# Key pages moved ahead of the prompt's attention, and the value pages interleaved with it, in a decoder-layer kernel

## What is computed

```
mod = silu(c) @ w_ada + b_ada                      # shift, scale, gate, twice
h = rms_norm(x) * (1 + scale1) + shift1
q, k, v, (GLA inputs), gates = h @ w_in
q, k = rms_norm per head                            # 8 heads of 64
prompt: softmax(q k^T * scale + rel_bias, causal) v # 512 x 512 per head, 4 blocks of 128 queries
sample: per sequence 2048 past keys and values in 16 pages of 128 tokens (page_table),
        + its own 4; a gate per block of 256 keys picks the top 3 past blocks; softmax; times v
o_g = gated linear attention (GLA), 4 heads, chunks of 32
x = x + gate1 * ((sigmoid(ga) * (o_a @ w_branch_a) + sigmoid(gb) * (o_g @ w_branch_b)) @ w_out)
x = x + gate2 * mixture of 32 experts (2 of them per token, SwiGLU)
```

## Time and profile before

| what | us |
|---|---|
| median of three runs | 1698.22 |
| the profiled execution, its own time | 1696.8 |
| its span | 1695.1 |
| prompt's attention, 176.8 to 288.3 | 111.5 |
| key pages, 288.3 to 389.6 | 101.3 |
| value pages, 389.6 to 456.1 | 66.5 |
| from there to GLA's first matmul, 460.0 | 3.9 |
| TensorE busy | 1493.1 (88%) |
| DMA, mean of the span | 224 GB/s |

### The profile page before, as it was taken

The page is one execution under the profiler, slowest core; times in us unless marked ns, Lnnn a source line. Parts: engine busy times, 40 slices in busy tenths (PEclk is TensorE's granted clock), DMA queues, the critical chain, the costliest instruction groups (busy, mean ns, idle before and its releaser), DMA issues.

```text
span 1695.1 us, 20005 instructions
## 1 busy us (share of the span) xinstructions
PE 1493.1 (88%) x7656; PEld 907.4 (54%) x7656; DVE 364.3 (21%) x845; ACT 296.7 (18%) x591; POOL 206.2 (12%) x283
## 2 busy tenths in 40 slices
PE   7899999999699999999999999858888888888880
PEld 4344455884285858585888878633333333333330
DVE  2432453032014141414000001431010101010104
ACT  3100322672022212131000000510000000000001
POOL 2121300334201010101000010010000000000006
PEclk9899656999699989899999999979888989898995
DMA  9954600999961222222131026339999999999984
GB/s 342 339 200 149 185 16 1 336 327 373 367 188 54 68 72 69 68 72 72 44 94 50 0 80 221 126 118 389 405 394 404 400 404 398 400 402 398 414 347 164
DMA packets 126621, 379.34 MB, mean 224 GB/s; under 512 B 9492, under 2 KB 54677, under 8 KB 110158
## 3 DMA queue, kind: packets, MB, share of 16 engines
q1 hardware_dynamic: 105552, 308.44, 48.7%
q0 software_dynamic: 20016, 67.11, 12.0%
q10 hardware_dynamic: 974, 2.74, 0.4%
HBM read 352.69 MB, written 25.56 MB: 223 GB/s over the span
## 4 chain that ended last, share of the span: by engine, by line
PE 28%; DMA 21%; DVE 2%; ACT 1%; issue 1%; POOL 0%; SPq 0%; POOLq 0%; ACTq 0%; DVEq 0%
PE ps L1279 28%; DMA ring<-in_w_exp_up 20%; PE ps L1290 1%; DVE work L1273 0%; ACT work L741 0%; DMA xT<-expert_rows,dest_i 0%; SPq L408 0%; DVE work L1272 0%; ACT hT L596 0%; DMA hT<-h_rows,idx 0%; DVE work L1104 0%; POOL work L570 0%; DMA expert_rows<-xT 0%; POOLq L108 0%; POOL work L566 0%
## 5 line engine op out<-in xcount | busy, mean ns | idle before, releaser
L1279 PE MATMUL ps<-ring,hT 128*64 128x512 f32 (+4 forms) x2416 | 628.9, 586 | 78.5 <-DMA ring<-in_w_exp_up 56.6
L1279 PEld LDWEIGHTS ps<-ring,hT 128*64 128x64 f32 (+2 forms) x2416 | 283.2, 160 | 398.0 <-issue 348.3
L1279 PE MATMUL ps<-work 128*32 128x128 f32 (+10 forms) x1812 | 227.1, 342 | 27.7 <-DVE work L1223 9.4
L1279 PE MATMUL ps<-hT,ring 128*128 128x272 f32 x768 | 187.5, 407 | 0.5 <-ACT work L718 0.5
L1279 PEld LDWEIGHTS ps<-work 128*32 128x32 f32 (+6 forms) x1812 | 137.8, 142 | 88.8 <-issue 29.6
L1279 PEld LDWEIGHTS ps<-hT,ring 128*128 128x128 f32 x768 | 151.6, 198 | 34.8 <-issue 1.5
L1279 PE MATMUL ps<-work,ring 128*128 128x272 f32 x640 | 148.2, 393 | 2.3 <-POOL work L525 2.3
L1279 PEld LDWEIGHTS ps<-work,ring 128*128 128x128 f32 x640 | 121.5, 190 | 27.7 <-POOL work L525 2.7
L769 ACT ACTIVATE hT<-ps 128x256 f32<-128x256 f32 x32 | 12.3, 384 | 451.2 <-PE ps L1279 451.2
L1290 PEld LDWEIGHTS ps<-cst,work 128*128 128x128 f32 (+5 forms) x388 | 52.0, 179 | 60.3 <-issue 45.9
L1290 PE MATMUL ps<-cst,work 128*128 128x128 f32 (+5 forms) x388 | 71.9, 312 | 12.6 <-DVE work L1039 4.5
(11 more groups left out here) (266 smaller groups left out, 924.9 us busy)
## 6 DMA issues: line engine op xcount, KB each, us to landing
ring<-in_w_exp_gate SPq DMA_DIRECT2D x32, 2048.0 KB, 19.0
ring<-in_w_exp_up SPq DMA_DIRECT2D x32, 2048.0 KB, 24.4
ring<-in_w_exp_down SPq DMA_DIRECT2D x32, 2048.0 KB, 24.6
ring<-in_w_ada SPq DMA_DIRECT2D x12, 2048.0 KB, 20.4
ring<-in_cache_k SPq DMA_DIRECT2D x64, 256.0 KB, 4.5
ring<-in_cache_k POOLq DMA_DIRECT2D x64, 256.0 KB, 4.7
ring<-in_cache_v SPq DMA_DIRECT2D x64, 256.0 KB, 6.9
ring<-in_cache_v POOLq DMA_DIRECT2D x64, 256.0 KB, 5.7
```

The source lines that it names most:

```text
L1279: return pe.matmul(out, lhsT, rhs, start=start, stop=stop, **k)
```

## The change

The stages are put in another order. The key pages follow the q/k/v tiles at once, in the same form as before. Then comes one loop over the prompt's 32 units, in which the value pages' blocks stand at fixed turns: blocks 1 to 7 behind the scores of turns 1, 3, ... 13 and blocks 8 to 15 behind those of turns 20, 22, ... 34; block 0 stands ahead of the loop. The transposes of the second group's weights stand at turns 15 to 19, one quarter each, and `selected(0)` at turn 20. The maximum of the second group is taken by VectorE ahead of the loop, its exponential by ScalarE ahead of the loop, its scaling by VectorE at turn 1. The projection `gk` goes behind the loop.

Ring slot 5 is left out of the pages' turns (`SPARE`), so pages use five slots; it holds `kpage` during the key stage, and then `sc_p` and the turned weights `prT`. The next block that SyncE puts into it (`AFTER_SPARE`) waits for the last transposes of the prompt and the last value block. The first 16 of POOL's page DMAs stand ahead of the stores of v. The remaining buffers are carved anew, and the PSUM banks are dealt out anew, since both stages are now alive at once.

```diff
-        SLOT_ORDER = [0, 1, 2, 3, 4, 5, 0] + [1, 2, 3, 1, 2, 3, 1, 2] + [3, 4, 1, 2, 5, 0] * 9
+        SLOT_ORDER = [0, 1, 2, 3, 4, 5, 0] + [1, 2, 3, 1, 2, 3, 1, 2] + [3, 4, 1, 2, 0] * 6 + [3, 4] + [1, 2, 0, 5, 3, 4] * 3
+        SPARE = 5
...
+        kpage = grid(ring[:, SPARE, :], 8)
+        sc_p, prT = grid(ring[:, SPARE, 0:3 * 512], 3), grid(ring[:, SPARE, 2048:], PAGES)
...
+        VALUES_AT = {**{2 * v - 1: v for v in range(1, 8)}, **{2 * v + 4: v for v in range(8, 16)}}
+        TURN_AT, SELECT_AT = 15, 20
...
+                if n == AFTER_SPARE:
+                    sp.wait_ge(s("p_tr"), 32)
+                    sp.wait_ge(s("pv_s"), 2 * PAGES // 2)
...
+            pool.wait_ge(s("page_table_in"), 16)
+            for i in range(4):
+                half_pages("k", i)
             pool.wait_ge(s("v_ready"), 5)
             pool.dma_start(v_prompt[0, 0]...)
             pool.dma_start(v_sample[0]...)
+            for i in range(4, KEY_PAGES // 8):
+                half_pages("k", i)
+            for i in range(KEY_PAGES // 8):
+                half_pages("v", i)
...
 # ScalarE
+            for pg in range(KEY_PAGES):        # page copies, exponent(0) among them
...
+            weights(0, range(5))
+            exponent(1)
             for x in range(34):                # the prompt's units
...
+                if TURN_AT <= x < TURN_AT + 5:
+                    weights(1, [x - TURN_AT])
+                if x == SELECT_AT + 1:
+                    sample_heads(0)
+            sample_heads(1)
...
 # VectorE
             for n in range(QUADS // 4):
                 dve.wait_ge(s("page_sc"), 4 * n + 4)
                 dve.tensor_copy(logits[n // 4][...], ps[:, 4 + n % 2, :]).then_inc(s("sc_taken"), 1)
+                if n == 5:
+                    softmax_norm(0)
                 if n % 4 == 3:
-                    softmax(n // 4)
+                    softmax_max(n // 4)
...
+            for x in range(32 + 4):            # the prompt's units
+                if x == 1:
+                    softmax_norm(1)
+                if x == TURN_AT:
+                    sample_rows(0)
+            sample_rows(1)
...
 # TensorE
-            pe.wait_ge(s("qk_T"), NORMED)
+            pe.wait_ge(s("pj_free"), NORMED)
             pe.wait_ge(s("v_ready"), 5)
+            for quad in range(QUADS + 1):      # the key pages, own_scores() behind quad 0
...
+            weights_turned(0, range(5))
+            page_values(0)
+            pe.wait_ge(s("sc_taken"), QUADS // 4)
             for x in range(32 + 3):
...
+                if x in VALUES_AT:
+                    page_values(VALUES_AT[x])
+                if TURN_AT <= x < TURN_AT + 5:
+                    weights_turned(1, [x - TURN_AT])
+                if x == SELECT_AT:
+                    selected(0)
...
+            product(2, lambda k: wgk[:, k, :], lambda k: hT[:, k, :], KD, RANK).then_inc(*done("gk_ps"))
             selected(1)
             pe.wait_ge(s("oa_taken"), 2)
+            pe.wait_ge(s("p_ov"), 32)
```

More of the change, by code:

```diff
@@ L49 @@
 TAB = 384
-WORK = 16550
+WORK = 16580
 RBM = 255
@@ L1399, in _, with own_scores @@
                     ada(ada_after(n))
-            pe.wait_ge(s("qk_T"), NORMED)
-            pe.wait_ge(s("v_ready"), 5)
+            def own_scores():
+                pe.wait_ge(s("qk_T"), NORMED)
+                pe.wait_ge(*after("q_row"))
+                for b in range(DEC_B):
+                    r = slice(32 * (b % 4), 32 * (b % 4) + 32)
+                    for a in range(PAIRS):
+                        last = mm(ps[r, 3, NS * (b // 4):NS * (b // 4) + NS], q_row[:, a, b, :], kT[:, a, sample], a == 0, a == PAIRS - 1,
+                                  skip_group_check=True)
+                last.then_inc(*done("own_ps"))
@@ new lines, in _ @@
+            pe.wait_ge(s("pj_free"), NORMED)
+            pe.wait_ge(s("v_ready"), 5)
+            for quad in range(QUADS + 1):
+                if quad < QUADS:
+                    for pg in range(4 * quad, 4 * quad + 4):
+                        n = PAGED[("k", pg // 8)]
+                        landed(pe, n)
+                        if pg >= 3:
+                            pe.wait_ge(s("page_T"), pg - 2)
+                        for a in range(PAIRS):
+                            last = turn(ps[:, pg % 3, P * a:P * a + P], slot(n)[:, AW * (pg % 8) + P * a:AW * (pg % 8) + P * a + P])
+                        last.then_inc(s("page_tr"), 1)
+                if quad == 0:
+                    own_scores()
+                if quad:
+                    y = quad - 1
+                    g, page = y // PAGES, y % PAGES
+                    pe.wait_ge(s("page_T"), 4 * y + 4)
+                    if y == 0:
+                        pe.wait_ge(s("mod_set"), 2)
+                    if page % 4 == 0 and y >= 8:
+                        pe.wait_ge(s("sc_taken"), y // 4 - 1)
+                    for a in range(PAIRS):
+                        for j in range(4):
+                            last = mm(ps[32 * j:32 * j + 32, 4 + y // 4 % 2, P * (page % 4):P * (page % 4) + P], q_row[:, a, 4 * g + j, :],
+                                      kpage[:, (4 * y + j) % 8, P * a:P * a + P], a == 0, a == PAIRS - 1, skip_group_check=True)
+                    last.then_inc(s("page_sc"), 1)
@@ new lines, in weights_turned @@
+            def weights_turned(g, part):
+                pe.wait_ge(s("l_norm"), g + 1)
+                for q in part:
+                    if q >= 2 or g:
+                        pe.wait_ge(s("pr_T"), 5 * g + q - (0 if g else 1))
+                    if q == 4:
+                        last = turn(ps[0:NS, 6 if g else 7, 0:P], logits[g][:, PAST:])
+                    else:
+                        for page in range(4 * q, 4 * q + 4):
+                            last = turn(ps[:, 6 if g else (6, 1)[q % 2], P * (page % 4):P * (page % 4) + P], logits[g][:, P * page:P * page + P])
+                    last.then_inc(s("pr_tr"), 1)
@@ new lines, in page_values @@
+            def page_values(v):
+                g, i = v // (PAGES // 2), v % (PAGES // 2)
+                if i == 0:
+                    pe.wait_ge(s("pr_T"), 5 * g + 5)
+                    if g:
+                        pe.wait_ge(s("o_rows"), g)
+                    for j in range(4):
+                        mm(ps[32 * j:32 * j + 32, 0, :], pr_own[0:NS, 32 * j:32 * j + 32], v_tok[0:NS, PT, :], True, False,
+                           skip_group_check=True)
+                n = PAGED[("v", v)]
+                landed(pe, n)
+                for page in (2 * i, 2 * i + 1):
+                    for j in range(4):
+                        q = 4 * (page % 2) + j
+                        last = mm(ps[32 * j:32 * j + 32, 0, :], prT[:, page, 32 * j:32 * j + 32], slot(n)[:, AW * q:AW * q + AW],
+                                  False, page == PAGES - 1, skip_group_check=True)
+                last.then_inc(s("pv_s"), 1)
@@ new lines, in selected @@
+            def selected(g):
+                pe.wait_ge(s("o_rows"), g + 1)
+                if g:
+                    pe.wait_ge(s("oa_taken"), g)
+                else:
+                    pe.wait_ge(s("pr_T"), 10)
+                for a in range(PAIRS):
+                    at = 64 * g + 16 * a
+                    last = mm(ps[:, 6, at:at + 16], o_rows[g][:, P * a:P * a + P], const("row_token"), True, True)
+                last.then_inc(s("o_sel"), 1)
+            weights_turned(0, range(5))
```

251 lines of the change are left out of this document (84 added, 167 removed).

## The result

The changed kernel took 1639.09 us, the median of four runs (1647.88, 1630.99, 1647.07, 1631.10), beside 1697.55 us for the kernel before on the same chip. The ratio is 0.9659, 95% interval 0.9589 to 0.9729: faster, by 58 us. The prediction said 1640. The runs fall into two groups, near 1631 and near 1647; the profiled one is of the longer group, 1647.88 us.

The account below looks back on a forecast made before the run. Bound: TensorE at half clock, TensorE at full clock, then DMA, in a row. Keys to 274.6, passage to 288.8, loop to 390.5, end to 401.4: 58.6 us off 1696.8, stated as 1640; 8-in-10 range 1619 to 1672.

Parts of the forecast that it names:

- The bound: Three stages in a row before GLA: TensorE at half clock, TensorE at full clock, DMA; together 283.2 us.
- Part 1, keys: Key stage, now first: 32 quads of 3.01 us plus 1.5 from 176.8, ending at 274.6, pages not binding.
- Part 2, the passage: Between keys and loop: second group's softmax delays the first transposes 14.2 us, to 288.8; TensorE idles some 5.
- Part 3, the loop: Units with value blocks among them: bound by TensorE, 101.7 us, ending at 390.5.
- the 89 and the quarter: Loop: 89 us if all at full clock; half clock taken for a quarter of the stage's time.
- the 7.4 of the sum: Loop: four units at full clock taken as 7.4 us, where before they repeated in 13.66 at half clock.
- The argument for the share: Loop: value blocks raise the clock and waits for pages lose it; blocks are near except at turns 14 to 19.
- Part 4, the end: Behind the loop, `gk` 7.27 us in the open, 10.9 in all; GLA starts at 401.4, 58.6 us earlier.
- The sum: Whole kernel: 1696.8 less 58.6 gives 1638.2 us, 1639.6 on the medians' scale, stated as 1640.
- Half clock all through (1713): Loop takes 168 us instead of 101.7, GLA starts 15.3 us later than before: 1713 us, chance 0.09.
- Turns that serialise: Loop: VectorE and ScalarE stand still behind each block, 114 us: 1652 in all, within the forecast's range, no own chance.
- Full clock from start to end: Loop takes 84 us, GLA starts at 383, gain 77 us: 1621 us, chance 0.17.

Follow-up runs that it names:

- Order alone: Changed kernel with key pages still first, but value blocks 1 to 15 and the second weights behind the units' loop: 1715.35 us, ratio 1.0096.
- Clock alone, in before: Kernel before with eight dense matmuls of resident data, result unread, at each odd turn of its attention loop: 1683.90 us, ratio 0.9916.
- kernel with `gk` early: Changed kernel with the `gk` projection moved from behind the loop to turn 1: 1630.95 us; measured a second time, 1628.42 us.
- thin ones: Changed kernel with one matmul of eight left in 12 of the value blocks, sample's results wrong: 1637.22 us, ratio 0.963.
- Spreading the turns: Changed kernel with the second weights' transposes at turns 5, 8, 12, 14, 15 and blocks 8 to 15 at turns 17 to 31: 1634.3 us.

## Why the prediction was right

**The bound.** Right: the units' 110 us at half clock were the cost, and the change took half clock away from them. Order alone: 1% slower. Clock alone, in before: GLA 18 us earlier, with 16 useless blocks in the stage. The other 33.7 us up to GLA are there only when the blocks are the useful ones and their pages move under the units; how much of them each of the two is worth was not taken apart.

**Part 1, keys.** Predicted 97.8 us to an end at 274.6; measured 100.0 (179.28 to 279.3), a quad 3.01 us as said, no wait for pages. The 2.2 us are the one wait of 2.28 us for ScalarE at 252.78. Of it 0.86 stood in before's key stage too, and 32 x 3.01 has no place for it; 1.42 is the table load, which I had not counted either: I moved the softmax's exponential but not the table it needs. The Trainium skill ("ScalarE: Activation LUTs", What ACT_TABLE_LOAD costs) gives 2.66 us for each switch, load and drain together; here the load's row is 1.28 us and the wait grew by 1.42. The stage also began 2.5 us later than 176.8, but this is the spread of executions: in the two other profiles of after it begins at 176.53 and 176.09.

**Part 2, the passage.** Predicted 14.2, measured 14.0 (279.28 to 293.33), with 5.0 us of TensorE idle as said. What I left out is that those waits cost the clock: three of three profiles of after lose it there for 6.8 us, as do all four others without `gk` in the gap, and with `gk` in it none of four did.

**Part 3, the loop.** Predicted 101.7, as 89 us at full clock with a quarter of the time at half; measured 104.3, with 30.7 us, 29%, at half. The kernel with `gk` early ran the same loop wholly at full clock in 90.4 us, so both the 89 and the quarter were low. A third term was too high and took back part of it: half clock was priced at half of its time, and it cost 13.9 us (104.3 less 90.4) for about 30, and 10.7 us for 23.8 between the two profiles of the `gk` kernel. Part of TensorE's waits vanish at the low clock. Four units alone at full clock keep TensorE busy for 7.52 us but take 8.58, with a wait of 1.01; in the loop, 90.4 less 25.2 for blocks and 4.5 for the rest leaves about 7.6 for four, near the 7.4 of the sum. So at full clock the blocks fill time that TensorE alone would spend in waits, and this makes the interleaved loop shorter than its parts one behind the other.

The argument for the share was half right. Blocks do bring the clock back: with them it rose after 3.4 to 17 us, without them not until the last unit, in up to 109 us. But they need not be dense, since thin ones do it too. What in them does it stays open. It is not that they fill waits: at half clock the units alone had hardly any (85.84 of 87.00 us busy) and stayed there. The places I named, turns 14 to 19, are where it was lost. The wait there is a queue: ScalarE's copy of the turned weights (L646) starts at 333.65, behind an exponential of 512 columns at 332.67 and its copy, while TensorE wants the bank it empties. Spreading the turns cut the wait to 0.76 us and the half-clock time to 10.2.

**Part 4, the end.** Predicted 10.9, measured 10.56 (397.64 to 408.20), `gk` 7.51 for 7.27. Behind GLA's start, 1238.0 us against 1235.1 in before, said to be unchanged: 2.9 us more. In the other profiles this same code took from 1236 to 1246 us. Its first 600 us are the same to 0.1 us of TensorE's work, so that the spread lies behind them, in the router and the experts. There the clock falls and rises every few tens of microseconds, and TensorE also waits for the experts' matrices from the DMA, 55.2 us in all in after and 74.8 with thin blocks, the longest tail, where TensorE itself was busy for 12 us less. So it is not the clock alone. In five of the six profiles in which GLA began before 400 us it took 1242 us or more, in all eight others less. What sets it was not traced, and it hides part of what was won in the loop: the spread turns began GLA 14.6 us earlier and ended 8.8 earlier.

**The sum** of the misses: 2.5 and 2.2 in front, 2.6 in the loop, 2.9 behind, against 0.5 given back in passage and end: 9.7 us; 1638.2 became 1647.9 in the profiled run. The median hit 1640 because half of the runs are 16 us shorter. The prediction had put its number on one profiled execution and did not foresee the two groups. That it hit within 1 us is therefore luck; that the gain is the clock and the interleaving, of about this size, is not.

**The rivals.** Half clock all through (1713) did not come; that the order alone gives 1715 is a coincidence, since that kernel has its blocks behind the units. Turns that serialise did not come either: TensorE idles 3.3 of 104.3 us, in two waits for ScalarE, and four units keep their 7.6 us. Full clock from start to end came in one profile of the `gk` kernel, with 90.4 us for the loop where the rival had 84. The Trainium skill ("TensorE: Matmul & The Clock Gate", Part 4) would have transposes not count as work: the key stage, two thirds transposes, held 1.00 for 101 us with the units far off, so that the rule does not decide here.

**Open.** Where the runs of about 1631 us differ from those of 1647 was not seen in after itself, as all three profiles are of the longer group. The two profiles of the `gk` kernel differ by 12.9 us in time, 10.7 of them in the loop, where one has 23.8 us at half clock and the other none; this is the likely answer. Why a wait of 1.74 us costs the clock in one execution and not in the next the traces do not show. The Trainium skill (same page, Part 1) says that the monitor behind the clock runs free of the kernel, so that the same program changes clock at other points; the two profiles agree with that and do not prove it.

## What to carry to other kernels

A stage in which TensorE is 99% busy at half clock may be one that could run at full clock: ask whether matmuls that stand in another stage behind the DMA can be put among its own. To find out, put useless matmuls among its work once and see whether it gets shorter. In a stage that holds the clock, a wait of 1 to 2 us costs its own length and, some of the time, more: 3.4 to 17 us at half clock followed here, and 23.8 us of them made one loop 10.7 us longer; look for these in the timeline beside the points where the clock falls, and fill them with independent matmuls or move what stands ahead of the copy that ends them. When a step is moved, move with it in the sum what it drags along, such as a table load.

## What was not expected of the hardware

- The same instructions have two steady rates: the prompt's units ran 49 us at 1.00 and then, in the same execution, 30 us at 0.50.
- Once at half clock, units with TensorE 96% busy (105.34 of 110.00 us) did not get it back before the last unit, 109 us later; with blocks of mostly one matmul every two turns they got it back in 17.
- A wait of 0.76 us, the longest inside its loop, was still followed by a drop, 2.6 and 0.7 us later in the two profiles that have it; in the units alone four waits of 1.01 us passed without one.
- At half clock TensorE's waits hide: the 1.01 us wait of full clock is 0.20 in the first round at half, so the low clock makes the engine look busier.
- 16 blocks of extra matmuls shortened a stage from 111.5 to 93.5 us.
